# Seven of a stage's fifteen units as plain fp32 products of unsplit weights, eight left in split form

## The reference

```python
cond = jax.nn.silu(c)
mod = cond @ ada_w[i, s] + ada_b[i, s]          # (1, 3*2048): shift, scale, gate
h = rms_norm(x, norm_g[i, 0]) * (1.0 + scale) + shift
b_gate, c_gate, v = jnp.split(h @ w_in, 3, axis=-1)      # w_in: 2048 x 6144
u = dwconv_centred(c_gate * v, w_conv)                   # width 3
x = x + gate * ((b_gate * u) @ w_out)
```

## Time and profile before

| | us |
|---|---|
| median of three runs | 2604.27 |
| the profiled execution, its time | 2604.66 |
| its span in the profile | 2602.9 |
| TensorE busy, matmuls | 2544.0 |
| VectorE busy | 2082.5 |
| ScalarE busy | 1377.1 |
| read from HBM | 675.58 MB |

### The profile page before, as it was taken

One profiled execution on the slowest core, in us unless ns is written; L12 is line 12 of the kernel. 1 busy time (PEld: TensorE's weight loads), 2 busy tenths in 40 slices (PEclk: granted clock), 3 DMA queues, 4 the chain that ended last, 5 costly groups with the idle time before them and its releaser, 6 DMA issues.

```text
span 2602.9 us, 45356 instructions
## 1 busy us (share of the span) xinstructions
PE 2544.0 (98%) x15582; PEld 2255.9 (87%) x15582; DVE 2082.5 (80%) x2637; ACT 1377.1 (53%) x2149; POOL 623.4 (24%) x576
## 2 busy tenths in 40 slices
PE   7899999999999999999999999999999999999998
PEld 6789999888888888888788888888888888888887
DVE  7988998998989989758788898888899655555654
ACT  4544454544444444556677645776754454444454
POOL 0011132333343343320011042113323111121123
PEclk8999999999999999999999999999999999999999
DMA  9979997798988888746565598554589555555554
GB/s 396 416 290 368 369 378 291 280 352 310 335 331 334 330 328 327 256 167 199 186 195 194 195 346 292 192 194 159 169 286 336 191 189 187 190 187 186 192 183 141
DMA packets 163918, 679.73 MB, mean 261 GB/s; under 512 B 18720, under 2 KB 18976, under 8 KB 139072
## 3 DMA queue, kind: packets, MB, share of 16 engines
q1 hardware_dynamic: 163728, 677.75, 72.6%
q0 software_dynamic: 48, 0.13, 0.0%
HBM read 675.58 MB, written 2.23 MB: 260 GB/s over the span
## 4 chain that ended last, share of the span: by engine, by line
PE 88%; DVE 6%; DMA 2%; ACT 1%; issue 1%; DVEq 0%; POOL 0%; ACTq 0%; POOLq 0%
PE psm L1159 47%; PE psm L1162 23%; PE psm L1225 3%; PE psm L1227 3%; PE psm L1226 3%; DVE wl L1475 2%; DMA xs<-in_ada 1%; PE psm L1440 1%; PE psr L1199 1%; DVE adat L1488 1%; ACT wh L730 1%; DMA raw<-in_w 1%; DVE xs L1488 1%; PE psr L1393 1%; PE psr L1440 1%
## 5 line engine op out<-in xcount | busy, mean ns | idle before, releaser
L1475 DVE TENSOR_TENSOR wl<-raw,wh 128x1024 fp32r<-128x1024 f32 x854 | 1079.6, 1266 | 289.9 <-ACT wh L730 285.1
L730 ACT ACTIVATE wh<-raw 128x1024 fp32r<-128x1024 f32 x854 | 900.4, 1056 | 388.6 <-PE psm L1162 179.3
L1159 PE MATMUL psm<-hcat,wh 128*128 128x512 f32 x3120 | 986.4, 397 | 1.4 <-DVE pad L1790 1.4
L1162 PEld LDWEIGHTS psm<-hcat,wl 128*128 128x128 f32 x3120 | 586.1, 188 | 138.6
L1159 PE MATMUL psm<-hid,wh 128*128 128x512 f32 x2240 | 703.6, 395 | 0.2 <-DVE wl L1475 0.2
L1162 PE MATMUL psm<-hcat,wl 128*128 128x256 f32 x3120 | 613.3, 278 | 0.0
L1162 PEld LDWEIGHTS psm<-hid,wl 128*128 128x128 f32 x2240 | 420.8, 188 | 99.5
L1159 PEld LDWEIGHTS psm<-hcat,wh 128*128 128x128 f32 x3120 | 476.1, 189 | 7.4 <-issue 5.9
L1488 DVE CUSTOM_DVE_ANT_0 adat<-adat,cond 128x2048 f32<-128x2048 f32 x176 | 462.8, 2630 | 16.0 <-DMA adat<-in_ada 15.9
L1162 PE MATMUL psm<-hid,wl 128*128 128x256 f32 x2240 | 440.0, 278 | 0.0
L1159 PEld LDWEIGHTS psm<-hid,wh 128*128 128x128 f32 x2240 | 341.0, 189 | 0.4 <-DVE wl L1475 0.4
(11 more groups left out here) (257 smaller groups left out, 2579.2 us busy)
## 6 DMA issues: line engine op xcount, KB each, us to landing
raw<-in_w SPq DMA_DIRECT2D x866, 512.0 KB, 4.4
adat<-in_ada SPq DMA_DIRECT2D x176, 1024.0 KB, 6.5
dec<-running_sums SPq DMA_DIRECT2D x48, 256.0 KB, 5.9
xs<-in_ada SPq DMA_DIRECT2D x8, 1024.0 KB, 11.3
zs<-in_ada SPq DMA_DIRECT2D x8, 1024.0 KB, 11.5
normt<-running_sums SPq DMA_DIRECT2D x16, 256.0 KB, 4.8
x<-in_xT SPq DMA_DIRECT2D x4, 512.0 KB, 9.6
out<-x SPq DMA_DIRECT2D x4, 512.0 KB, 3.5
```

Of the source, the lines that this page charges most:

```text
L730: act.activation(wh[:, h % 4, :], raw[:, h % 4, :], ACT.Copy).then_inc(hi_done, 1)
L1159: pe.matmul(both, wh[:, h % 4, (k + i) * P:(k + i + 1) * P], src[:, kb + i, :, :], start=(kb + i == 0), stop=(kb + i == KB - 1), skip_grou ...
L1162: mm = pe.matmul(bank[:, T:2 * T], wl[:, h % 4, (k + i) * P:(k + i + 1) * P], src[:, kb + i, 0, :], start=False, stop=(kb + i == KB - 1), ...
L1475: dve.tensor_tensor(wl[:, h % 4, :], raw[:, h % 4, :], wh[:, h % 4, :].bitcast(F32), ALU.subtract).then_inc(lo_done, 1)
```

## The change

Seven of the fifteen head units (c0, v0, c1, v1, c2, v2, c3: n = 0 to 6) are computed as one plain fp32 matmul per block, `raw` against `hv` (h before it is split), in place of three fp32r passes. Their 112 blocks stand in 14 slabs of their own ("whole" slabs), which ScalarE and VectorE pass over. The other eight units' 128 blocks stand in 16 slabs, one for each channel block, split as before. The new order of the 30 slabs is: for channel blocks 0 to 6 a split slab and then a whole one; for 7 a split one alone; for 8 to 14 split, then whole; for 15 split. A whole slab begins in one channel block and ends in the next. The number of slabs, their bytes and their places in SyncE's queue stay the same. Three waits change: a slab four behind a whole one is loaded when that whole one is multiplied (`mm_done`); TensorE waits for `h_full` and `raw_in` before plain products, and for `h_lo` and `lo_done` only before the split ones; ScalarE, before it overwrites one of the four slots of `hv`, waits until the channel block four before has been multiplied.

```diff
+WHOLE = 7
+WHOLE_BLOCKS = [(kb, n) for kb in range(KB) for n in range(WHOLE)]
+HEAD_STREAM, HEAD_WHOLE = [], set()
+for _kb in range(KB):
+    HEAD_STREAM.append([(_kb, n) for n in range(WHOLE, HEAD_UNITS)])
+    for _p in range(len(WHOLE_BLOCKS) // 8):
+        if WHOLE_BLOCKS[8 * _p][0] == _kb:
+            HEAD_WHOLE.add(len(HEAD_STREAM))
+            HEAD_STREAM.append(WHOLE_BLOCKS[8 * _p:8 * _p + 8])
+HEAD_PLACE = {b: (h, k) for h, slab in enumerate(HEAD_STREAM) for k, b in enumerate(slab)}
...
-                at_least(sp, mm_done if unsplit(h - 4) else lo_done, h - 3)
+                at_least(sp, mm_done if unsplit(h - 4) or whole(h - 4) else lo_done, h - 3)
                 sp.dma_start(raw[:, h % 4, :], w[h.v]).then_inc(raw_in[h % 4], 16)
...
+                if whole(h):
+                    at_least(act, hi_done, h)
+                    act.sem_inc(hi_done, 1)
+                    return
...
                 if k >= 4:
                     at_least(act, h_lo, k - 3)
+                    act.wait_ge(mm_done, HEAD_PLACE[k - 4, WHOLE][0] + 1)
...
-                for i in range(KB * HEAD_UNITS):
-                    kb, n = divmod(i, HEAD_UNITS)
-                    if i % 8 == 0:
-                        at_least(pe, lo_done, i // 8 + 1)
-                    if n == 0:
-                        at_least(pe, h_lo, kb + 1)
-                    mm = block(head_bank[n // 2][:, (n % 2) * T:(n % 2) * T + T], i // 8, i % 8,
-                               hcat[:, kb, 0, :], hcat[:, kb, 1, :], kb == 0 and n % 2 == 0, kb == KB - 1)
-                    if i % 8 == 7:
-                        mm.then_inc(mm_done, 1)
+                for kb in range(KB):
+                    for n in range(HEAD_UNITS):
+                        h, k = HEAD_PLACE[kb, n]
+                        sums = head_bank[n // 2][:, (n % 2) * T:(n % 2) * T + T]
+                        first, after = kb == 0 and n % 2 == 0, kb == KB - 1
+                        if n == 0:
+                            at_least(pe, h_full, kb + 1)
+                        if n == WHOLE:
+                            at_least(pe, h_lo, kb + 1)
+                            at_least(pe, lo_done, h + 1)
+                        if n < WHOLE:
+                            if k == 0:
+                                pe.wait_ge(raw_in[h % 4], h // 4 * 16 + 16)
+                            mm = pe.matmul(sums, raw[:, h % 4, k * P:(k + 1) * P], hv[:, kb % 4, :], start=first,
+                                           stop=after, skip_group_check=True)
+                        else:
+                            mm = block(sums, h, k, hcat[:, kb, 0, :], hcat[:, kb, 1, :], first, after)
+                        if k == 7:
+                            mm.then_inc(mm_done, 1)
...
+                if whole(h):
+                    at_least(dve, lo_done, h)
+                    dve.sem_inc(lo_done, 1)
+                    return
```

More of the change, by code:

```diff
@@ L102, in unsplit, with whole @@
     return not h.terms and h.c in UNSPLIT
+def whole(h):
+    return not h.terms and h.c in HEAD_WHOLE
 def behind(g):
@@ L2035 @@
     head = np.asarray(sc_in_w[0]).reshape(KB, P, 3, KB, P)
-    head = np.stack([head[kb, :, "bcv".index(part), j] for kb in range(KB) for part, j in HEAD_ORDER])
+    head = np.stack([head[kb, :, "bcv".index(HEAD_ORDER[n][0]), HEAD_ORDER[n][1]]
+                     for slab in HEAD_STREAM for kb, n in slab])
     head = head.reshape(-1, 2, 8, P, P).transpose(0, 1, 3, 2, 4).reshape(-1, 2, P, HALF)
```

## The result

The median after is 2609.51 us (20 runs, 2606.9 to 2612.16), against 2604.66 for the kernel before in the same job (20 runs, 2603.38 to 2607.05): a ratio of 1.0018 [1.0011, 1.0024], so 4.85 us slower. The prediction was 2605.3 with a range of 2603.4 to 2608.5: the time lies above it, on the side of rival 1. The profiled execution took 2609.45 us with a span of 2607.7 (2602.9 before).

The account below looks back on a forecast made before the run. The prediction took the DMA transfers to bound the head. Removed 0, added 1.0 us (0.9 at the head's end, 0.1 for T31): 2604.66 + 1.0 = 2605.7 profiled, 2605.3 median, range 2603.4 to 2608.5.

Parts of the forecast that it names:

- rival 1: Head transfers: DMA engines run dry where TensorE falls behind and frees slots late; +2 to +5 us, 2608; chance 14%.
- the slots are held longer: Head slab slots: freed only after their plain products; worst late case S28 delays T31 0 to 0.2 us, 0.1 counted.
- The end of the head: Head's end: S32 waits for the seventh plain product, issued at 138.8, so the first c copy starts 0.9 us later.
- VectorE's and ScalarE's relief: Head: 14 slabs no longer split, 17.1 us off VectorE and 14.8 off ScalarE; valued at nothing, at most 0.25 us.
- TensorE's 8.3 us: Head on TensorE: plain products add 8.3 us of work, none on the path, with 1.6 us slack per channel block.
- Rival 2: Head: TensorE becomes the bound if plain products alternating with fp32r passes cost 0.87 us; +22 us, 2627; chance 7%.
- The early slots: Head's front: S5 waits for channel block 1's plain products, issued between 33.7 and 35.8 us; 0 to 1.0 lost, taken 0.

Follow-up runs that it names:

- early slabs free: Changed kernel, but plain products of S1 to S13 read a constant block, so those slots aren't held: 2610.24 us against 2604.6 before, 1.0022.
- S32 freed: Changed kernel, but plain products of S28 alone read a constant block, so S32 doesn't wait for TensorE: 2610.24 us against 2605.32 before, 1.0022.
- gate at h: Changed kernel, S16 to S28 replaced by a constant block, but S20, S22, ... S30 issued only when their channel block's h is ready: 2607.7 against 2605.32 before.
- wait put behind more: Changed kernel, all slots held, every head slab one place later in the order of SyncE, ScalarE and VectorE: 2605.84 us against 2605.32 before, 1.0003.
- late slabs free: Changed kernel, but plain products of S16 to S28 read a constant block, S1 to S13 still held: 2604.3 us against 2604.6 before, 1.0.
- order pair: Head slabs one place later in the order, in the changed kernel (2605.84 us) and in the kernel before (2603.99), each against 2605.32 before.
- nothing held: Changed kernel, but all plain products read a constant block, so slots fall free as before the change: 2605.1 us against 2604.6 before, 1.0001.

## Why the prediction was wrong

**The step that failed** is in "the slots are held longer": "1.75 pass before its own bytes count. 1.8 against 1.75: T31 comes 0 to 0.2 us later". The lead of 1.8 came true, in part by luck: S28 is issued 1.9 us before T29 lands (VectorE takes T29 at 126.46), because two misses cancel: the gate opened 0.5 us later than forecast, and T29 came 8.15 us after T27 and not 7.53, by the loss at the gate before. What such a lead costs was wrong, and so was counting one gate. I took 1.75 us from the quickest landing of a slab in the whole trace, which is one that meets idle engines, and asked it of one gate only, the narrowest. The table has all gates of the late head, in the kernel after and in the runs with the early slabs free, S32 freed, the gate at h and the wait put behind more. The lead is read to the start of the last tile's sum; where VectorE was busy when the tile landed, it is a little less than stated. The loss is even tile to even tile, less 7.53.

| gates | lead, us | loss, us |
|---|---|---|
| S28, S32 freed | 0.2 | 2.9 |
| S28, S28, S26 | 1.8, 1.9, 1.9 | 1.7, 1.35, 0.6 |
| S26 | 2.1, 2.25 | 1.0, 0.5 |
| S22 | 2.6, 2.8, 2.8 | 1.0, 1.1, 1.4 |
| S20 and S24, six gates | 3.0 to 3.6 | 0 to 0.2 |
| S20, S22, S26, S28, gate at h | 3.8, 3.8, 3.8, 4.1 | 0, 1.8, 0, 0.5 |
| S24, gate at h; all with the wait put behind more | 5.1 and more | 0 to 0.1 |

In the kernel after every gate with less than 3 us lost, S22's, S26's and S28's (leads of 2.6, 2.1, 1.9), and S24's at 3.4 hardly did. Their losses of 1.0, 1.0, 1.35 and S24's 0.2 are the 3.6 at T31. So the step put 0 to 0.2 us at S28 where 1.35 was lost, and nothing at S22, S24 and S26 where 2.2 were lost together. 1.75 was too little: at S26 and S28 even 2.25 us of lead was not enough. A fixed need it is not. S22's place lost 1.0 to 1.8 in all four runs with a gate there, more at a lead of 3.8 than at 2.6, and S28's lost 0.5 at 4.1. That the late issue costs there is shown (with the late slabs free it costs nothing); that the size of the lead decides how much is not, and what makes S22's place dear is open.

**A term mis-sized beside it.** The gate was put at 3.5 + j x 0.434 us after the landing, 5.7 for S28. Measured is 124.51 - 118.31 = 6.2: a quarter of a microsecond more before TensorE's first product (122.05 against 118.31 + 3.5) and 0.3 from the end of the fifth to the issue, both left out. With 0.5 more the lead at S28 would have been 2.4, still where the table has losses, so this alone could not have saved the forecast.

**The end of the head** came out by its own steps: S32 is issued 142.44 - 135.38 = 7.06 us after T31's sum starts (forecast 138.8 - 131.8 = 7.0) and lands in 3.3 (forecast 3.0 to 4). From T31's sum to the copy it is 11.33 us against 10.86 before, +0.5 where I had +0.9; the order pair gives 1.2, so between 0.5 and 1.2 it is not better known.

**VectorE's and ScalarE's relief, valued at nothing**: right within what the run with nothing held can tell. The splits' busy time fell by 15.8 us on VectorE and 15.1 on ScalarE, and VectorE first waits for a tile at 41.6 us (forecast 45).

**TensorE's 8.3 us, hidden**: right. Its busy time rose by 8.2. The last block's plain products, and the first split one behind them:

```profile
139.12 1.99 PE L1270 MATMUL psm<-normt,raw 128*128 128x256 f32 x8 [1.68 <-ACT normt L821]
140.95 1.46 PE L1270 MATMUL psy<-normt,raw 128*128 128x256 f32 x6
142.06 0.47 PE L1245 MATMUL psy<-hcat,wh 128*128 128x256 f32 x1
```

Seven take 142.06 - 139.12 = 2.94 us, 0.42 each (forecast 0.434). Rival 2 is out: products of the two kinds alternating cost what each costs alone.

**The early slots, 0 to 1.0 lost, taken as 0**: right. S5 is issued at 33.69, the best end of my 33.7 to 35.8, T22 stands at 97.95 against 97.86 before, and the run with only the late slabs free shows no loss.

**Rival 1** named the right result, a dry queue and 2608 us, from 90 us on, but made it depend on TensorE falling behind at a low clock. The clock was full in the profile from 90 to 140 us, and the sign that I had set for this rival, a DMA share under 0.95, came (0.89 from 110 to 120 us); the slack was too small without a fall of the clock. The chance of 14% was wrong for the same reason as the sum: with a need bounded from above by a loaded landing as well as from below by the idle one, "1.8 against 1.75" would have been a term of 0 to several microseconds, and it fell due at every late gate (three lost 1 us or more), not at one.

## What to carry to other kernels

When a change makes a request wait for compute, count for every such gate how much is still in the queue when it opens, and compare it with a loaded transfer's start and landing, not with the quickest landing in the trace: here gates with less than 3 us of queue lost 0.5 to 2.9 us each, three of them added up, and only from 5 us on was none seen to lose. Putting the gates behind one more transfer brought the change's cost down from 4.85 to 1.85 us here, so the order of requests is worth trying before the change is dropped. Work saved on engines that wait for the transfers was worth nothing here, and a slot held longer for it had a price.

## What the runs showed that I had not expected

The DMA engines' share fell to 0.04 while the last tile still took 1.3 us or more to land, so "in flight until its landing" overstates what keeps them busy. Holding the same slots with split slabs cost 34.5 us against 4.85: the gates opened 3 us later (8.1 against 4.9 at S22), the early ones cost too, and TensorE's granted clock fell (0.67 from 130 to 140 us).
